# Hybrid pooling / gated DeltaNet block: the input projection as seven half-size products, weight sums added by DMA, and re-timed hand-overs

## The reference, cut to what matters

```python
D_MODEL, SEQ, N_META, POOL_WIDTH, DN_WIDTH, DN_HEADS, DN_HEAD_DIM, CHUNK = 2048, 512, 16, 1024, 2048, 16, 128, 64
h = concatenate([meta, x], axis=1)                       # 528 tokens
xn = rmsnorm(h, norm_w)
proj = xn @ w_in                                         # 2048 -> 14368 columns
u_pool, z_pool, q, k, v, z_dn, b, a, gate_pool, gate_dn = split(proj)
y_pool = (causal_multiscale_pool(u_pool, pool_mix, pool_scale) * silu(z_pool))
# gated DeltaNet: conv of 4 taps + silu on q, k, v; l2norm of q and k; per head and chunk:
decay = where(causal, exp(gcum_i - gcum_j), 0)
tmat  = inverse(eye + strict(k_beta @ k.T * decay))      # then u, w, qk, a scan over chunks with a state
y_dn  = rmsnorm(o, norm_w) * silu(z_dn)
merged = sigmoid(gate_pool) * (y_pool @ w_pool_out) + sigmoid(gate_dn) * (y_dn @ w_dn_out)
out = rmsnorm((h + merged @ w_o)[:, N_META:], final_norm_w)
```

## Time and profile before

| what | value |
|---|---|
| median of 3 runs | 1962.52 us (1961.95 to 1963.54) |
| span of the profiled execution, first to last instruction | 1960.8 us |
| TensorE busy | 1931.4 us (99%) |
| VectorE busy | 921.4 us (47%) |
| ScalarE busy | 726.0 us (37%) |
| GpSimd busy | 78.3 us (4%) |
| stage A starts on PE / one pair of heads / gates end | 35.8 us / 115.7 us / about 1518 us |

### The profile page before, as it was taken

How to read it: one execution, slowest core, us unless ns; L and a number is a source line. 1 busy time by engine, 2 the same in 40 slices (tenths; PEclk the granted TensorE clock), 3 DMA queues, 4 the chain that set the end, 5 groups by cost and what they waited for, 6 DMA issues and landing times.

```text
span 1960.8 us, 35753 instructions
## 1 busy us (share of the span) xinstructions
PE 1931.4 (99%) x13729; PEld 1724.3 (88%) x13729; DVE 921.4 (47%) x2315; ACT 726.0 (37%) x2136; POOL 78.3 (4%) x105
## 2 busy tenths in 40 slices
PE   5999999999999999999999999999999999999998
PEld 5888899999999999999999988888888888888886
DVE  6333343656556466555646654322224444335332
ACT  5422223435353443535345353323234322224232
POOL 4000000000000000000000000000000000000000
PEclk8999999999999999999999999999999999999999
DMA  6133342433333242333334144333443534347302
GB/s 222 59 103 102 102 134 88 119 95 86 95 120 90 87 124 69 96 111 100 91 107 123 44 131 127 119 107 128 134 162 134 186 118 139 118 139 279 108 22 86
DMA packets 221302, 225.73 MB, mean 115 GB/s; under 512 B 33665, under 2 KB 197978, under 8 KB 220522
## 3 DMA queue, kind: packets, MB, share of 16 engines
q1 hardware_dynamic: 158898, 180.17, 28.1%
q10 hardware_dynamic: 55944, 22.63, 4.6%
q0 software_dynamic: 6336, 21.08, 3.4%
HBM read 199.65 MB, written 25.30 MB: 115 GB/s over the span
## 4 chain that ended last, share of the span: by engine, by line
PE 97%; ACT 1%; DVE 1%; issue 0%; POOL 0%; DMA 0%; ACTq 0%; SPq 0%; DVEq 0%
PE pj L530 82%; PE pg L530 10%; PE pt L530 3%; PE pt L679 1%; PE pg L781 0%; POOL xl L1696 0%; DVE fst L1233 0%; ACT xsquare L908 0%; DMA xt<-in_meta_tokens 0%; PE pj L574 0%; DVE xl L1239 0%; ACT wh L868 0%; DVE xt L1246 0%; ACT L1041 0%; ACT L1070 0%
## 5 line engine op out<-in xcount | busy, mean ns | idle before, releaser
L530 PE MATMUL pj<-xh,wh 128*128 128x512 f32 (+3 forms) x2688 | 735.1, 328 | 3.2 <-DVE wl L1208 3.1
L530 PE MATMUL pj<-xh,wl 128*128 128x512 f32 (+3 forms) x2688 | 712.4, 319 | 0.0
L530 PE MATMUL pj<-xl,wh 128*128 128x512 f32 (+3 forms) x2688 | 712.3, 319 | 0.0
L1208 DVE TENSOR_TENSOR wl<-raw,wh 128x256 fp32r<-128x256 f32 x896 | 344.2, 421 | 603.0 <-ACT wh L868 601.5
L530 PEld LDWEIGHTS pj<-xh,wh 128*128 128x128 f32 x2688 | 446.9, 189 | 43.2 <-DVE wl L1208 3.4
L530 PEld LDWEIGHTS pj<-xh,wl 128*128 128x128 f32 x2688 | 448.4, 188 | 35.9
L530 PEld LDWEIGHTS pj<-xl,wh 128*128 128x128 f32 x2688 | 448.8, 189 | 33.9 <-issue 1.0
L868 ACT ACTIVATE wh<-raw 128x256 fp32r<-128x256 f32 x896 | 307.0, 410 | 64.7 <-issue 45.0
L868 ACT ACTIVATE wh<-rawb 128x256 fp32r<-128x256 f32 (+1 forms) x224 | 85.0, 437 | 217.0 <-PE pj L530 189.8
L530 PE MATMUL pj<-yl,wh 128*128 128x512 f32 x384 | 149.5, 389 | 0.0
L530 PE MATMUL pj<-yh,wl 128*128 128x512 f32 x384 | 149.5, 389 | 0.0
(11 more groups left out here) (243 smaller groups left out, 1784.3 us busy)
## 6 DMA issues: line engine op xcount, KB each, us to landing
raw<-in_w_in SPq DMA_DIRECT2D x112, 1024.0 KB, 6.2
rawb<-in_w_dn_out SPq DMA_DIRECT2D x16, 1024.0 KB, 6.3
rawb<-in_w_o SPq DMA_DIRECT2D x12, 1024.0 KB, 5.3
gates_scratch<-stg ACTq DMA_DIRECT2D x32, 256.0 KB, 2.1
rawb<-in_w_pool_out SPq DMA_DIRECT2D x8, 1024.0 KB, 5.7
gst<-gates_scratch POOLq DMA_DIRECT2D x32, 256.0 KB, 3.1
yraw<-branch_scratch SPq DMA_DIRECT2D x1, 5632.0 KB, 23.1
xt<-in_x SPq DMA_DIRECT2D x4, 1024.0 KB, 6.2
```

The source lines that it names most:

```text
L530: return pe.matmul(dst, lhs, rhs, start=start, stop=stop)
L1208: tt(wl[:, j, 2 * q:2 * q + 2, :], raw[:, 2 * par + h, 2 * q:2 * q + 2, c * P:(c + 1) * P], wh[:, j, 2 * q:2 * q + 2, :].bitcast(F32), ALU ...
```

## The change

**Seven products.** Tokens are taken in two halves of 264 (8 meta tokens and 256 each), the inner dimension in two halves of 8 tiles, the block's 256 columns in two tiles. A block is computed as seven products of halves (Strassen's scheme in Winograd's form), each of 8 tiles x 3 terms over 264, 260 or 256 tokens. `xh`, `xl` now hold seven operands (four sums of quarters among them), made at the start by DVE, with their high parts by ACT. The order in a block is `(7, 6, 2, 5, 4, 3, NEXT)`; NEXT is product 1 of the following block. A chunk is half a product (4 tiles, 12 matmuls), 14 chunks a block.

**Sums of weights.** Of a block's four raw quarters (1024 rows x 512 B, 512 KB each) SP loads four; two further quarters are *added* to a buffer by transfers that POOL issues with `accum_op=ALU.add` (`s3_addition`, `s4_addition`); two sums (`s1`, `s2`, 128x1024) are made by DVE. Splits are now 128x512, 14 a block, four chunks ahead of PE.

**Sums of results.** ACT copies three intermediate states of the banks (`snap`), DVE makes `c21`, `c22`, `c11` of 264 columns; ACT takes the last quarter from PSUM.

**Delta rule.** Heads are convolved in two tiles `stg`, SiLU applied at once, and stored to HBM (`head_store`, 8 a pair); SP loads them back (`load_kq`, `load_vch`, `load_zst`). ACT makes the first tap. POOL makes the whole argument of the decay (difference, times a 0/1 mask, plus a mask: three operations of 128x1024). POOL issues the transfers of the blocks (`blocks_out`, `inverses_back`). The evacuations of steps L0 to L0+5 move from DVE to ACT. Steps are one a chunk, 56 a pair; DVE does two columns of the inverse a step.

**Stage B** begins with `rawb` loaded when the last block starts; `yraw` is loaded in five parts during the gate blocks.

```diff
+ORDER_FIRST = (1, 2, 7, 6, 4, 5, NEXT, 3)
+ORDER = (7, 6, 2, 5, 4, 3, NEXT)
+ORDER_LAST = (7, 6, 2, 5, 4, 3)
+AHEAD = 4
+RINGS = 5
...
-        G0 = 3
+        G0 = 2
         F0 = G0 + 2
         V0 = F0 + 4
-        W0 = F0 + 9
-        NSTEP = 3
+        W0 = F0 + 8
+        NSTEP = 2
...
-        L0 = W0 + 15
+        L0 = W0 + 17
...
+            def block_loads(b, par, col, between=None):
...
+                    sp.wait_ge(lo_done, base + after(order, 2))
+                    load_raw(buffer_of(b, par, 2), 21, col)
+                    sp.wait_ge(lo_done, base + after(order, 5))
+                    load_raw(RA, 11, col)
+                    if between == "kq":
+                        load_kq(between_pair[0])
+                    sp.wait_ge(lo_done, base + after(order, 4))
+                    load_raw(RF, 22, col)
+                if between == "z":
+                    load_zst(between_pair[0])
+                sp.wait_ge(lo_done, base + after(order, 3))
+                load_raw(buffer_of(b, par, 3), 12, col)
...
+            def block_products(b, par, kind, kind_next, hook):
...
+                for i, what in enumerate(order):
+                    if what == 7:
+                        need(pe, add_done, added(b - 1, "C21"))
+                    elif what == 6:
+                        pe.wait_ge(snap_done, snapped(b, "s1"))
+                    elif what == 4:
+                        pe.wait_ge(snap_done, snapped(b, "s4"))
+                    elif what == 2:
+                        need(pe, add_done, added(b - 1, "C11"))
+                    elif what == 5:
+                        pe.wait_ge(snap_done, snapped(b, "s2"))
+                    elif what == NEXT:
+                        need(pe, last_done, b)
+                    elif what == 3:
+                        pe.wait_ge(add_done, added(b, "C22"))
...
+                        pe.wait_ge(lo_done, base + chunk + 1)
+                        for k in range(HK):
+                            kt = HK * h + k
+                            for w, xx, one, last in ((wh, xh, True, False), (wh, xl, False, False), (wl, xh, False, True)):
+                                mm = pe.matmul(bank[:, c0:TH], w[:, slot, k, :], xx[what][:, kt, c0:TH],
...
+            def block_steps(b, par, kind, dst, free, event, hook, early=None):
...
+                    if not first and t == 8:
+                        free(1)
+                        c22(b, par, kind, dst[1])
+                    if early is not None:
+                        early(t)
+                    for of, par_of, at in split_targets(b, par, t):
+                        split_lo(of, par_of, at)
...
+                    if not first and t == 0:
+                        s1(b, par)
+                    if not last and t == (14 if first else 12):
+                        s2(b + 1, 1 - par)
...
+                    if t == 10:
+                        c21(b, kind, dst[1])
...
+                    event(t)
...
+                    hook(2 * t)
+                    hook(2 * t + 1)
...
+            def add_quarter(slot, quarter, b, added_to):
+                r, c = KH * P * (quarter in (12, 22)), column_of(b) + P * (quarter in (21, 22))
+                pool.dma_start(raw[:, slot, :, :], w_in[0, r:r + KH * P, c:c + P].rearrange("(k p) c -> p k c", p=P),
+                               accum_op=ALU.add).then_inc(added_to, 16)
+
+            def s4_addition(b):
+
+                pool.wait_ge(sum_done, summed(b, "S1"))
+                pool.wait_ge(lo_done, base_of(b) + after(order_of(b), 6))
+                add_quarter(buffer_of(b, b % 2, 3), 12, b, s4_added)
+
+            def s3_addition(b):
+
+                pool.wait_ge(raw_loaded[buffer_of(b, b % 2, 7)], 16 * b + 16)
+                add_quarter(buffer_of(b, b % 2, 7), 11, b, s3_added)
...
+            def blocks_out(d):
+
+                pool.wait_ge(mk_ready, d + 1)
+                pool.dma_start(full_rows(gram_d), slots(mk)).then_inc(mk_stored, 16)
+                pool.dma_start(blocks(gram_d, NBLK - 2, NBLK).rearrange("a j c -> j a c"), tail(mk)).then_inc(mk_stored, 16)
+                pool.wait_ge(mk_stored, 32 * d + 32)
+                pool.wait_ge(norm_sum, d + 1)
+                pool.dma_start(gblk, blocks(gram_d, 0, NBLK)).then_inc(blk_loaded, 16)
+
+            def inverses_back(d):
+
+                pool.wait_ge(w_turned, d + 1)
+                pool.wait_ge(blk_zeroed, 32)
+                pool.dma_start(blocks(inv_d[1], 0, NBLK), wtr).then_inc(wtr_stored, 16)
+                pool.dma_start(blocks(inv_d[0], 0, NBLK), wblk).then_inc(wblk_stored, 16)
+                pool.wait_ge(wtr_stored, 16 * d + 16)
+                pool.dma_start(slots(tm), full_rows(inv_d[1])).then_inc(tm_loaded, 16)
...
+            for d in range(PAIRS):
+                for k in range(4):
+                    b = CP_PAIR0 + 4 * (d + 1) + k
+                    s4_addition(b)
+                    if k == 3 and d < PAIRS - 1:
+                        row_load(d + 1)
+                    s3_addition(b + 1)
+                    if k == 3 and d < PAIRS - 1:
+                        differences(d + 1)
+                    if k == 0:
+                        blocks_out(d)
+                    if k == 1:
+                        inverses_back(d)
+                    if k == 3:
+                        head_out(d)
```

More of the change, by code:

```diff
@@ L74, with base_of, order_of, buffer_of @@
 NGATE = 2 * D // CW
-CB = 512
-NCB = D // CB
 NCP = CP_GATE0 + NGATE
+RA, RB, RE, RF = range(4)
+def base_of(b):
+    return 0 if isinstance(b, int) and b == 0 else 14 * b + 2
+ALL_CHUNKS = base_of(NCP - 1) + 2 * len(ORDER_LAST)
+def order_of(b):
+    if isinstance(b, int):
+        return ORDER_FIRST if b == 0 else ORDER_LAST if b == NCP - 1 else ORDER
+    return ORDER
+def buffer_of(b, par, product):
+    if product == 5:
+        return RF if isinstance(b, int) and b == 0 else RA
+    return {1: RA, NEXT: RA, 2: (RB, RE)[par], 3: (RE, RB)[par], 4: RF, 6: (RE, RB)[par], 7: (RE, RB)[par]}[product]
+def after(order, product):
+    return 2 * order.index(product) + 2
 CI = 0
@@ new lines, in hook, with first_tap @@
+                    def hook(h, z=z):
+                        if tables and table_step(h) is not None:
+                            table_acts(z, table_step(h))
+                    block_acts(b, z, POOL_KINDS[z], ("zp", "k")[z], event, hook)
+            pool_blocks(0, True, False)
+            pool_blocks(1, False, True)
+            with act.Fori(2, GROUPS) as g:
+                pool_blocks(g, False, False)
+            def first_tap(p, k, c):
+                b = CP_PAIR0 + 4 * p + k
+                if c == 1:
+                    act.wait_ge(add_done, added(b, "second"))
+                    if k == 0:
+                        act.wait_ge(conv_cur, p + 1)
+                        act.wait_ge(zeroed, 2)
+                else:
+                    act.wait_ge(last_done, b + 1)
+                need(act, head_stored[c], 16 * (4 * p + k))
+                act.activation(stg[:, c, :], xin[:, 3:3 + T], ACT.Copy, scale=convcur[:, 3, (1, 0, 2)[k], c:c + 1]).then_inc(conv_step, 1)
@@ new lines, in by_slot @@
+                def by_slot(bank, size):
+                    return bank[:, 0:SLOTS * size].rearrange("p (i c) -> p i c", c=size)
+                if m == L0:
+                    wait(x_mm, 3, 1)
+                    act.activation(xm, by_slot(pg[0], BS), ACT.Copy, scale=odd).then_inc(x_ready, 1)
+                if m == L0 + 2:
+                    wait(x_mm, 3, 2)
+                    for first, second in PAIRED:
+                        copy(xm5[second], by_slot(pg[0], 2 * BS)[second]).then_inc(x_ready, 1)
@@ new lines, in _, with no_event, gate_block, free @@
+            pair_blocks(0, None)
+            with dve.Fori(1, PAIRS) as p:
+                pair_blocks(p, p - 1)
+            def no_event(t):
+                return None
+            def gate_block(i, par, event, hook):
+                def free(c):
+                    if isinstance(i, int) and i == 0:
+                        dve.wait_ge(head_stored[c], 16 * 4 * PAIRS)
+                    else:
+                        dve.wait_ge(gate_stored[c], 16 * i)
+                block_steps(CP_GATE0 + i, par, "gate", [stg[:, c, :] for c in range(2)], free, event, hook)
@@ L1725, in _ @@
[L1725 to L1735 removed]
+            s3_addition(1)
```

1359 lines of the change are left out of this document (854 added, 505 removed).

## The result

The median went from 1962.9 us (4 runs, 1962.0 to 1963.5) to 2084.3 (4 runs, 2078.6 to 2087.8): a ratio of 1.062, 95% interval 1.060 to 1.064. The profiled execution has a span of 2076.9 us, where the sum of the prediction gives 1876.8. 200 us have to be found.

A forecast was written before the change was run, and what follows sets the result against it. PE's matmuls, one after another, were taken to bound the kernel. The terms -135.6 + 6.5 + 3 + 40 + 2 gave -84 us, so 1960.8 becomes 1876.8 profiled, 1878 median, range 1840 to 1940.

The forecast's parts named there:

- The products: All projection blocks: 168 half-wide matmuls instead of 96 per block save 135.6 us of PE time.
- Rival 4: PE's matmuls: columns don't get cheaper, a 264 at 0.137 us, so products save nothing, 2014 us; chance 0.03.
- Added quarters: Weight sums by adding transfers, every block: they land in time, 0 us; bounds 0 and 5 us in each of 56 blocks.
- 9.4: Gate block: us the addition s4 has from wait to landing before ACT needs it for PE's chunk 10 at 14.1.
- rival 3: Added quarters late at ACT's chunk 10 copy, slower from 10.9 us; chance 0.07 beyond threshold, 0.02 at it, 0.05 mild.
- a budget of 11.5 us: Gate block: time the addition s3 has, starting when quarter 21 has landed, near 7 us.
- Waits in a pair: Eight delta-rule pairs: PE waits 5 us in each, 40 in all; bounds 1 and 12 a pair.
- the 2.5: Pair, steps 12 to 18: PE's wait for DVE's crowded work, with c11 behind s1 before product 2, 2.5 us.
- The first block: Start: DVE's sums, low parts and splits end the first block near 67 against 60.5, +6.5 us; bounds 0 and 12.
- The tables: Gate tables on ACT: PE waits for the first snapshot of the next block, +3 us; bounds 0 and 7.
- GpSimd's decay argument: POOL's operations, ordered a block ahead of ACT's exponential: 0 us; if late, 0 to 1 us a pair.
- Stage B: Last block: DVE's low parts, splits and chunks take about 19.6 us against 17, +2 us; bounds 0 and 5.

The follow-up runs named there:

- plain_transfers: Changed kernel with both added transfers of a block overwriting instead of adding, same queue and pieces: 1986.8 us, ratio 1.011.
- no_additions: Changed kernel without both added transfers, their waits replaced by waits for the load or sum before: 1961.2 us, ratio 1.000.
- no_s3_addition: Changed kernel without the addition that makes S3, that of S4 kept: 2015.4 us, ratio 1.027.
- c22_first: Changed kernel with DVE making c22 before the low parts of chunks 10 and 11 instead of behind them: 2055.8 us, ratio 1.047.

## Why the prediction was wrong, point by point

- **The products, -135.6: right.** A gate block without waits takes 19.88 us (forecast 19.8), 21.8 before. Rival 4 is out.
- **Added quarters, 0: the step that failed.** Measured 123 us, 36 of them in the gate blocks, where the cause is shown. Three sizes in it were off. s1 ended at 4.6 us and GpSimd issued at 4.9 (3.4). The hand-over from ACT's copy to PE took 2.4 us (1.3), since c22 stood behind two low parts. Quarter 21 landed at 10.0 us, for the "near 7" from which S3's budget was counted. The landing, 8.7 us, was inside the 5.8 to 9.2 that I gave (issuing took GpSimd 1.55 us of it, for 2.0), but 9.4 was no longer the budget: it was 14.2 - 4.9 - 2.4 = 6.9. (The 6.3 us of `plain_transfers` are under it, and ten of its twelve gate blocks take 19.9.) So rival 3 had the right place, and its threshold was 2.5 us too high. And it had one loop. S3's, which I dismissed with a budget of 11.5 us, closes on itself over the load of quarter 21: 4.7 us of load, 8.8 of addition, 8.1 of chunks, s2 and s1. A budget against PE doesn't show this; only going round the loop does. The longest landing was 13.9, against the bound of 14.4.
- **Waits in a pair, 5: too small even without additions.** A pair took 117.4 in `no_additions`. The prediction's own rows add up to 105.3 without waits (81.0 for the four blocks and 24.3), not 104.9, so the waits, with the clock behind them, took 12.1, my upper bound of 12. The list of PE's waits there has 68 us for eight pairs, 8.5 each; 27 us of the eight ran at the lower clock, half of it lost, 1.7 a pair. The other 2 us a pair are assigned to nothing. The first of the list:

```profile
PE pj L744 <- ACT snap L1069: 17.9, 13, 2.8
PE pj L744 <- DVE xin L1619: 10.9, 7, 1.8
PE pj L744 <- DVE wl L1555: 10.5, 10, 1.7
PE pg L709 <- DMA st<-inverse_scratch: 9.4, 7, 3.2
```

  Snapshots are first. One of them stands behind ACT's exponential and its table load, which I had counted in ACT's busy time but not as a wait; it is 1.15 us for PE in this pair, and nearly the same in the seven others:

```profile
698.22 1.28 ACT L1275 ACT_TABLE_LOAD   x1
699.51 1.06 ACT L1275 ACTIVATE dec<-dec 128x1024 f32<-128x1024 f32 x1
700.48 0.21 ACT L1276 ACTIVATE dec<-dec 16x32 f32<-16x32 f32 x1
700.60 0.36 ACT L1069 ACTIVATE snap<-pj 128x264 f32<-128x264 f32 x1
```

  Then c11 behind s1, which I named inside the 2.5; DVE's low parts; the way back of the inverses, 1.2 a pair, where I said 1. DVE's busy time in a pair, 85 forecast, was 86.0 (87.8 without additions). The average was right. I take the order for what made the waits; the one edit of it that was tried here, c11's, moved them. With the additions a pair took 123.6, and 68.3 us of the eight at the lower clock, half of it lost, are 4.3 of it.
- **The first block, +6.5: about 6 short.** It ended at 73.5 without additions; PE began at 35.6 instead of 32. With them at 81.6, since S3 for block 1 was late as well (73.2 in `no_s3_addition`).
- **The tables, +3: short by 3.** PE waited 5.8 us for the snapshot in block 3, with the additions and without them, inside the bounds of 0 to 7. (The 6.9 us in that sum are 6.5 by its own rows.)
- **GpSimd's decay argument, 0:** no wait of PE's names it. It was not tried by itself.
- **Stage B, +2: right within 1 us, by another way.** Without the additions the last block took 19.2 us for its 17. But in `c22_first` it took 17.9: the 2 us were c22's place behind DVE's other work, not DVE's work in all.
- **The clock was in no term.** It took at most 62 us of the 121 by which the kernel got slower.

Pairs and start as forecast would not have saved the direction: by the measured parts that is some 66 us of 2084, about 2018 (an estimate), still slower than 1963. With the additions as forecast, at nothing, the kernel would not have been faster either (1961). What the seven products save, the waits in pairs, start and tables took back (1961 for 1963), and the added quarters came on top.

## What to carry to other kernels

Where a tile is made anew in each round from what the last round released, add up the loop itself (release, load, landing, sum, copies, release) and compare it with the round's length: a loop over 100% bounds the kernel however early each piece seems against the bottleneck engine, and with two such loops the repair of one alone shows little. An adding transfer is priced by work, twice a copy's, and by landing under the load of the real kernel. And a kernel whose PE never waited has its clock for nothing; the first idle stretches cost more than their length.

## What the runs showed that I had not expected

- An adding transfer of 512 KB in 512-byte rows lands in 6.4 us alone and 9.0 (6.5 to 13.9) in the kernel; a plain one from the same queue in 4.5 and 5.4. The adding one is 1040 packets, the plain one 144. A plain one from SP's queue, also of 1040 packets, lands in 3.9.
- 256 KB adding: 4.6 us alone, 7.8 in the kernel. Halving it gained 1.2 us there.
- GpSimd's 128x1024 additions cost DVE more (1.5 us each) than they would take on DVE (1.2).
- Stretches at the lower clock at or behind some of PE's waits, down to a wait of 1.7 us (in one place, two waits of 0.8 us shortly one behind the other): 25 between the first block and the end of the projection in the profiled execution. Where such waits were filled with products, there was none.
